# Eight shift rows of the first modulation on TensorE, one column at a time, and four moves on DVE and SP

## What is computed

```python
cond = jax.nn.silu(c)
for l in range(DEPTH):
    m = (cond @ w_mod[l] + b_mod[l]).reshape(bsz, 3, 3, D_MODEL)     # [sublayer, (shift, scale, gate)]
    x = x + 0.5 * m[:, 0, 2][:, None] * swiglu(adaln_in(x, norm_g[l, 0], m, 0), ...)
    h = adaln_in(x, norm_g[l, 1], m, 1) @ w_in[l]
    # mixer: 8 heads of attention beside a short or long convolution, then w_out with gate m[:, 1, 2]
    # second feed-forward with m[:, 2, :]
def adaln_in(x, g, m, i):
    return rmsnorm(x, g) * (1 + m[:, i, 1][:, None]) + m[:, i, 0][:, None]
```

## Time and profile before

| | us |
|---|---|
| median of 3 runs | 1430.19 (1429.68 to 1430.36) |
| profiled execution, its own time | 1432.25 |
| its span | 1430.5 |
| PE busy / PEld busy | 1358.0 / 1294.1 |
| DVE busy / ACT busy | 1088.9 / 692.5 |
| DMA, mean | 213 GB/s |

### The profile page before, as it was taken

One profiled execution on the slowest core, in us unless ns is written; L12 is line 12 of the kernel. 1 busy time (PEld: TensorE's weight loads), 2 busy tenths in 40 slices (PEclk: granted clock), 3 DMA queues, 4 the chain that ended last, 5 costly groups with the idle time before them and its releaser, 6 DMA issues.

```text
span 1430.5 us, 26076 instructions
## 1 busy us (share of the span) xinstructions
PE 1358.0 (95%) x10734; PEld 1294.1 (90%) x10734; DVE 1088.9 (76%) x1835; ACT 692.5 (48%) x1120; POOL 53.9 (4%) x57
## 2 busy tenths in 40 slices
PE   2899999899999999999998999999999989999998
PEld 2899998799999989999998789999997868899998
DVE  6788998887787879888778766565578767677776
ACT  3343435555344354334464544443477756554453
POOL 0000000002000000001000020000010021100000
PEclk9999999999999999999999999999999999999999
DMA  9898758346877576574653055545432325244551
GB/s 393 344 404 324 295 192 325 117 151 274 331 275 295 222 297 267 223 295 191 271 209 138 32 205 205 222 177 214 161 142 84 139 65 186 87 180 177 183 195 65
DMA packets 32182, 305.79 MB, mean 214 GB/s; under 512 B 3480, under 2 KB 5784, under 8 KB 7360
## 3 DMA queue, kind: packets, MB, share of 16 engines
q1 hardware_dynamic: 32064, 304.13, 55.0%
HBM read 303.05 MB, written 1.06 MB: 213 GB/s over the span
## 4 chain that ended last, share of the span: by engine, by line
PE 85%; DVE 6%; ACT 3%; DMA 3%; issue 2%; POOL 1%; SPq 0%; POOLq 0%; DVEq 0%; ACTq 0%
PE bank L690 14%; PE bank L694 14%; PE bank L691 14%; PE bank L864 13%; PE bank L783 7%; PE bank L781 7%; PE bank L788 7%; DMA ring<-in_stream 2%; DVE WL L1856 2%; PE bank L673 1%; PE bank L708 1%; DMA PR<-in_stream 1%; PE bank L937 1%; ACT WH L1283 1%; PE bank L957 1%
## 5 line engine op out<-in xcount | busy, mean ns | idle before, releaser
L1856 DVE TENSOR_TENSOR WL<-ring,WH 128x1024 fp32r<-128x1024 f32 x414 | 495.9, 1221 | 64.2 <-ACT WH L1283 62.1
L1283 ACT ACTIVATE WH<-ring 128x1024 fp32r<-128x1024 f32 x414 | 424.5, 1054 | 145.2 <-DMA ring<-in_stream 55.0
L690 PE MATMUL bank<-XH,WH 128*128 128x256 f32 x1648 | 403.3, 283 | 4.3 <-ACT WH L1283 4.3
L691 PE MATMUL bank<-XL,WH 128*128 128x256 f32 x1648 | 401.5, 282 | 0.0
L690 PEld LDWEIGHTS bank<-XH,WH 128*128 128x128 f32 x1648 | 311.5, 189 | 10.2 <-issue 9.7
L691 PEld LDWEIGHTS bank<-XL,WH 128*128 128x128 f32 x1648 | 311.4, 189 | 0.5 <-issue 0.5
L694 PE MATMUL bank<-XH,WL 128*128 128x256 f32 x1648 | 230.1, 282 | 0.0
L694 PEld LDWEIGHTS bank<-XH,WL 128*128 128x128 f32 x1648 | 210.7, 189 | 0.0
L781 PE MATMUL bank<-GH,WH 128*128 128x256 f32 x840 | 202.6, 279 | 0.1
L783 PE MATMUL bank<-GL,WH 128*128 128x256 f32 x840 | 202.5, 279 | 0.0
L1368 ACT ACTIVATE SG<-bank 128x256 f32<-128x256 f32 x84 | 32.2, 384 | 334.7 <-PE bank L694 330.2
(11 more groups left out here) (321 smaller groups left out, 1601.4 us busy)
## 6 DMA issues: line engine op xcount, KB each, us to landing
ring<-in_stream SPq DMA_DIRECT2D x128, 1536.0 KB, 6.7
scr<-in_stream SPq DMA_DIRECT2D x15, 1536.0 KB, 11.1
PR<-in_stream SPq DMA_DIRECT2D x15, 1536.0 KB, 9.3
att<-in_stream SPq DMA_DIRECT2D x15, 1536.0 KB, 10.0
ring<-in_stream SPq DMA_DIRECT2D x13, 1024.0 KB, 5.0
ring<-in_stream SPq DMA_DIRECT2D x10, 512.0 KB, 3.6
kf_mix<-in_stream SPq DMA_DIRECT2D x2, 1536.0 KB, 16.8
con<-in_consts SPq DMA_DIRECT2D x1, 1680.0 KB, 14.8
```

Of the source, the lines that this page charges most:

```text
L690: pe.matmul(o, part(WH, u, k), XH[:, k, :], start=(k == 0), stop=False)
L691: pe.matmul(o, part(WH, u, k), XL[:, k, :], start=False, stop=False)
L1283: act.activation(part_all(WH, u), raw(u), ACT.Copy).then_inc(*mark("high", u))
L1856: dve.tensor_tensor(part_all(WL, u), raw(u), part_all(WH, u).bitcast(F32), ALU.subtract)\
```

## The change

- Input: the front items are packed otherwise. Scale row k is row 2k, shift row k is row 2k+1, and a shift row now holds eight 128x128 blocks with the condition's features on the partitions. Rows 16 and 17 are the gate rows. `c_cols` holds the condition as eight columns.
- SP: X, the ones and ring slot 0 are issued first, then the 16 rows one by one, the later ones when the row six places before has been read; then the gate rows, into the place of item 0. The waits of mod items 6 and later and of ring slot 2 are on the new marks.
- TensorE: `shift(k)` makes 128 shift values by eight products with one moving column; ACT adds `b_mod`. Products of chunk 0 are made for each k between the shifts. The `keep_warm` calls of the front go.
- DVE: 8 scale rows instead of 16 rows; the norm goes chunk by chunk. The gate rows are read behind the first gating.
- Ends of feed-forwards: DVE's rows of `mod_rows(f, 20, 1)` and the memsets come behind the last gating; `down(21)` waits for it one product later.
- Attention: layer 0's `conv_unit(7)` (but its factor) and `conv_unit(8)`, layer 1's `short_conv(12)`, `z_mul(2)` and two WL splits come behind the first maxima or first probabilities.

```diff
+
+    def front_row(n):
+
+        a = (n % MOD_ROWS) * D
+        return mod_slots[n // MOD_ROWS][:, a:a + D]
+
+    def front_read(i):
+
+        n = range(MOD_ROWS * i, min(MOD_ROWS * (i + 1), 2 * KD))
+        scales, shifts = [j // 2 for j in n if j % 2 == 0], [j // 2 for j in n if j % 2 == 1]
+        gates = [("mod_read", HEAD_MODS - 1)] if i == 0 else []
+        return [("scale_in", k) for k in scales[-1:]] + [("shift_sum", k) for k in shifts[-1:]] + gates
...
+            sp.dma_start(con[:, 0:2 * P], const_d[:, 0:2 * P]).then_inc(*mark("ones_in", n=16))
+            sp.dma_start(X, x_d).then_inc(*mark("x_in", n=16))
+            first = ("ffn", 0, 0)
+            sp.dma_start(slot(first), stream[ITEM_AT[first], :, 0:COLS[first]]).then_inc(sig.sem("slot_landed0"), 16)
+            for j in range(2 * KD):
+                if j >= FRONT:
+                    sp.wait_ge(*at("shift_sum" if j % 2 else "scale_in", (j - FRONT) // 2))
+                a = (j % MOD_ROWS) * D
+                sp.dma_start(front_row(j), stream[ITEM_AT["mod", j // MOD_ROWS], :, a:a + D]).then_inc(*mark(f"mod_landed{j % FRONT}", j, n=16))
+            sp.wait_ge(*at("scale_in", 1))
+            sp.wait_ge(*at("shift_sum", 0))
+            sp.dma_start(mod_slots[0][:, D:ITEM], stream[ITEM_AT["mod", HEAD_MODS - 1], :, D:ITEM])\
+                .then_inc(*mark("gate_rows_in", n=16))
...
+                if name == first or name[0] == "mod" and name[1] < HEAD_MODS:
+                    continue
...
-                        sp.wait_ge(*at("mod_read", p))
+                        for w in front_read(p) if p < HEAD_MODS else [("mod_read", p)]:
+                            sp.wait_ge(*at(*w))
+                        if p < HEAD_MODS:
+                            j = max(j for j in range(2 * KD) if j % FRONT == k)
+                            sp.wait_ge(*at("shift_sum" if j % 2 else "scale_in", j // 2))
...
-                    for k in range(KD):
+                    def shift(k):
+                        take(k % 2, "shift_in", k)
+                        pe.wait_ge(*at(f"mod_landed{(2 * k + 1) % FRONT}", 2 * k + 1))
+                        if k == 0:
+                            pe.wait_ge(*at("c_cols"))
+                        for d in range(KD):
+                            last = pe.matmul(bank[k % 2][:, 0:1], front_row(2 * k + 1)[:, d * P:(d + 1) * P], prm("c_cols", d),
+                                             start=(d == 0), stop=(d == KD - 1))
+                        last.then_inc(*mark("shift_sum", k))
+
+                    def products(k):
                         pe.wait_ge(*at("norm_high", key, k))
                         for a, u in units:
-                            if k == 0:
-                                pe.wait_ge(*at("high", u))
-                            pe.matmul(b[:, a * S:(a + 1) * S], part(WH, u, k), XH[:, k, :], start=(a == 0 and k == 0), stop=False,
-                                      skip_group_check=True)
-                    for a, u in units:
...
+                            for which, w in ((WH, ("high", u)), (WL, low_of(u))):
+                                if k == 0:
+                                    pe.wait_ge(*at(*w))
+                                pe.matmul(b[:, a * S:(a + 1) * S], part(which, u, k), XH[:, k, :],
+                                          start=(which is WH and a == 0 and k == 0), stop=False, skip_group_check=True)
+
+                    def low_products(k):
...
+                    for k in range(KD):
+                        shift(k)
+                        if k > 0:
+                            products(k - 1)
+                        if k > 1:
+                            low_products(k - 2)
+                    products(KD - 1)
+                    low_products(KD - 2)
+                    low_products(KD - 1)
+
...
-                    pe.wait_ge(*at("gated", f, c))
+                    if f == 4 or c < NFF - 1:
+                        pe.wait_ge(*at("gated", f, c))
...
@@ -1613,9 +1654,35 @@
             act.wait_ge(*at("par_in"))
             act.wait_ge(*at("c_in"))
             act.activation(cond[:, :], cond[:, :], ACT.Silu).then_inc(*mark("cond"))
+            act.activation(prm("c_cols", 0, 8), prm("c_cols", 0, 8), ACT.Silu).then_inc(*mark("c_cols"))
+
+            def front_norm():
+                k0, (u0, u1) = ("sub", 0, 0), up_units(0, 0)
+                load_rates()
+                squares(k0, lambda c: [("x_in",)])
+                split_to(u0)
+                root(k0)
+                split_to(u1)
+                for k in range(KD):
+                    act.wait_ge(*at("scale_in", k))
+                    g = prm("norm_g", k)
+                    act.activation(adav[:, 0, 0, k:k + 1], modv[:, KD + k:KD + k + 1], ACT.Identity, scale=g, bias=g)\
+                        .then_inc(*mark("rate_in", k))
+                    act.wait_ge(*at("shift_sum", k))
+                    act.activation(modv[:, k:k + 1], bank[k % 2][:, 0:1], ACT.Identity, bias=prm("b_mod", k))\
+                        .then_inc(*mark("shift_in", k))
+                    if k > 0:
+                        if k == 1:
+                            act.wait_ge(*at("shift_in", 0))
+                        act.wait_ge(*at("shift_in", k - 1))
+                        highs(k0, [k - 1])
+                act.wait_ge(*at("shift_in", KD - 1))
+                highs(k0, [KD - 1])
+                split_to(u1)
+
             for l in range(2):
                 if l == 0:
-                    norm(("sub", 0, 0), lambda c: [("x_in",)], ahead=up_units(0, 0)[1])
+                    front_norm()
                 else:
                     norm(("sub", 1, 0), added("ffn1"), ahead=up_units(2, 0)[1] + 1)
...
@@ -1990,6 +2054,15 @@
                     ends = f < 4 and c == NFF - 1
                     if not ends:
                         split_to(up_units(f, c)[1] + PARTS)
+                    if f == 0 and c == 0:
+                        dve.wait_ge(*at("gate_rows_in"))
+                        for r in range(1, MOD_ROWS):
+                            mod_row(HEAD_MODS - 1, r)
+                    if ends:
+                        mod_rows(f, c - 1, 1)
+                    if ends and f != 1:
+                        link(dve.memset(PR[:, :, 0:PADL], 0.0))
+                        link(dve.memset(PR[:, :, PADL + S:PW], 0.0))
                     mod_rows(f, c, 0)
                     if f == 0:
                         start_step(c)
@@ -1997,10 +2070,8 @@
                         filter_step(c)
                     if c > 0 and not ends:
                         split_to(UNIT_AT["w2", f, c - 1] + PARTS)
-                    mod_rows(f, c, 1)
-                    if f in (0, 2, 3) and c == NFF - 2:
-                        link(dve.memset(PR[:, :, 0:PADL], 0.0))
-                        link(dve.memset(PR[:, :, PADL + S:PW], 0.0))
+                    if f == 4 or c != NFF - 2:
+                        mod_rows(f, c, 1)
...
-            for i in range(HEAD_MODS - 1):
-                for r in range(MOD_ROWS):
-                    mod_row(i, r)
-            mod_row(HEAD_MODS - 1, 0)
-            scale_rates(0, 0)
-            norm_root(("sub", 0, 0))
+
+            def scale_row(k):
+                dve.wait_ge(*at(f"mod_landed{2 * k % FRONT}", 2 * k))
+                w = front_row(2 * k)
+                dve.tensor_tensor_reduce(w, w, cond[:, :], 1.0, prm("b_mod", KD + k), ALU.mult, ALU.add,
+                                         accum_out=modv[:, KD + k:KD + k + 1]).then_inc(*mark("scale_in", k))
+
+            def front_norm():
+                k0, (u0, u1) = ("sub", 0, 0), up_units(0, 0)
+                scale_row(0)
+                split_to(u0)
+                scale_row(1)
+                split_to(u1)
+                norm_root(k0)
+                for k in range(1, KD + 1):
+                    if 1 < k < KD:
+                        scale_row(k)
+                    dve.wait_ge(*at("rate_in", k - 1))
+                    norm_scale(k0, [k - 1])
+                    if k > 1:
+                        norm_lows(k0, [k - 2])
+                norm_lows(k0, [KD - 1])
+
             for l in range(2):
                 if l == 0:
-                    norm_parts_of(("sub", 0, 0), lambda: split_to(up_units(0, 0)[1]))
+                    front_norm()
                     split_to(up_units(0, 1)[1])
-                    dve.wait_ge(*at("gate_rows_in"))
-                    for r in range(1, MOD_ROWS):
-                        mod_row(HEAD_MODS - 1, r)
...
@@ -2242,13 +2327,19 @@
                     split_to(u0 + 6 + PARTS)
                     head_scale("a")
 
+                    def factor(j):
+                        c, role = conv_role(j)
+                        g = PR[:, 11 + c, :]
+                        dve.wait_ge(*at("act_copied", name, j - 1))
+                        dve.wait_ge(*at("product", name, j))
```

(28 more changed lines are left out.)

53 lines of the change are left out of this document (23 added, 30 removed).

## The result

| | before | with the change |
|---|---|---|
| median, us | 1430.28 (1429.68 to 1431.40, 4 runs) | 1438.01 (1437.04 to 1438.74, 4 runs) |
| ratio | | 1.0048 [1.0033, 1.0063] |
| profiled execution, span | 1432.25, 1430.5 | 1438.74, 1436.9 |
| PE busy / PEld busy | 1358.0 / 1294.1 | 1382.2 / 1320.5 |
| mean granted clock | 0.989 | 0.98 |

What follows compares the result with a forecast made beforehand. TensorE was taken to bound the kernel, with 85% of the chain. The terms +0.7 - 3.1 - 2.3 - 4.9 = -9.6 us took the runs' median from 1430.19 to 1420.6, range 1416 to 1434.

Steps and rivals of the forecast that it cites:

- front: Start of the kernel up to chunk 2: chunk 2 at 58.7 instead of 58.0 us, +0.7 (bounds -2.5 and +3).
- ends, maxima of both layers: Work moved behind last gatings and first maxima or probabilities: -3.1, -2.3 and -4.9, together -10.3 us.
- a step: Front, one shift row plus products of chunk 0: 3.4 us at full clock, 5.8 in the first rival.
- The first rival: Clock falls during the front's one-column shift rows: step 5.8, chunk 2 +14.7, total 1434.6 us; chance 0.22.
- The second rival: Front clock falls but weight loads keep their price: step 4.1, chunk 2 +3.5, total 1423.4 us; chance 0.10.
- The load behind the front: Modulation item 6 and ring slot 1 queue from 35.8; chunk 1 starts at 47.6 (was 42.14), slow clock costs 2.6.
- Ends of feed-forwards: Last chunks' gating: TensorE's three waits of 3.3 us go but for one hop each, -3.1 us (bounds 0 and -3.3).
- First maxima: Attentions' first turns start sooner: layer 0 -2.3 us (bounds -1.0, -5.6), layer 1 -4.9 (bounds -1.5, -5.2).

Runs made afterwards that it cites:

- front_only_pad: The changed kernel's front alone, ends of feed-forwards and first maxima as before, with eight more unused parameter columns than the changed kernel: 1428.06 us, ratio 0.9977.
- before_pad16: The kernel before with sixteen unused parameter columns, every tile behind the parameters 64 bytes further: 1417.81 us, ratio 0.9902.
- moves: The kernel before with only the ends of feed-forwards and the first maxima of both attentions moved as in the change: 1421.87 us, ratio 0.9928.
- before_pad: The kernel before with eight unused parameter columns, tiles behind them 32 bytes further: 1435.41 us, ratio 1.0021.
- wide: after_pad with 128 moving columns in each shift product in place of one: 1408.24 us, ratio 0.9835.
- after_pad: The changed kernel with eight more, unused parameter columns: 1417.79 us, ratio 0.9903.
- after: The changed kernel itself, with the whole change against the kernel before: 1438.01 us, ratio 1.0048.
- xh32: The kernel before with eight unused parameter columns and the key norms' tile behind GL, so XH, XL move 32 bytes and GH, GL stay: 1425.21 us.
- ring2_x128: wide with ring slots 1 and 2 issued earlier, tiles behind the parameters 128 bytes further than in the kernel before: 1415.64 us, ratio 0.9889.
- before_g64: The kernel before with sixteen unused parameter columns and an unused sixteen-column tile ahead of SG, GH, GL: 1402.18 us, ratio 0.9799.
- ring2_g64: wide with ring slots 1 and 2 issued earlier and an unused sixteen-column tile ahead of SG, GH, GL: 1394.57 us, ratio 0.9734.

## Why the prediction was wrong, step by step

| term | forecast | measured | from |
|---|---|---|---|
| front | +0.7 | +10.3 | front_only_pad, before_pad16 |
| ends, maxima of both layers | -10.3 | -10.4 | moves |
| 32 bytes | none | +3.1 (profiles: +6.0) | before_pad |

The forecast's sum was -9.6, and the two steps that it lacks are the slow clock in the shift rows (without it the front is +0.8, by `wide`) and the tiles that the new columns push on.

**The front** is the step that failed. "In the new order TensorE does shift(k), then products(k-1)" was right, and "a step is 1.83 + 0.9 + 6 x 0.118 = 3.4" was right for the clock that it assumed (3.49 in `wide`). The reason why it should have that clock was not: I read from the rows that the clock falls behind idle times of 3.7 us and more, and took a TensorE that stands only 0.9 at a time to be safe. It fell at 18.3 with no idle time since TensorE's first product at 9.91. `after_pad` has the same fall; `wide` differs from it in the moving columns alone and keeps the clock up through the same waits. So it was the one-column products. The first rival had the mechanism and its sizes: 3.5 for a shift row (3.41), a step of 5.8 (5.60). It was 3.6 too high at chunk 2 (11.1 for 14.7): the up-projection of chunk 0 ended near 57.6 where it had 61.6, of which seven shorter steps are 1.4, and some 22 records that ran before the clock fell, 0.1 cheaper each, are 2.2. I gave it 0.22; with no row of one-column work longer than 1.9 us, it should have had more.

The second rival (loads keep their price) is out. By the rule of the Trainium skill that the prediction weighed (TensorE: Matmul & The Clock Gate, LDWEIGHTS: columns over 1.2, one figure) a load would take the same at both clocks; these traces have 333 ns at 0.50 (`after`, above) and 192 at 1.00 (`wide`).

**The load behind the front** was forecast from a front that didn't come: in the changed kernel ring slot 1 is there when ACT splits it, from 54.87 on, and TensorE doesn't wait at 57.59. In `wide` it came nearly as worked out: item 6 and slot 1 issued at 35.52 and 35.90 (forecast 35.8), chunk 1 at 46.65 (47.6), the slow clock behind it; the front's term is 1408.24 less (1417.81 - 10.4), +0.8 for +0.7.

**Ends of feed-forwards**: -1.55, -1.35 and the third one's share; forecast 3.1 together. **First maxima**: layer 0 -2.2 (forecast -2.3), layer 1 with the third end -5.2 (forecast 4.9 and about 0.5). The reasons hold: idle time of 1.4 and 0.9 us ahead of the turns (1.2 and 1.1 forecast), no slow clock behind them, small waits in layer 0 (0.89 for the conv gate) that give a part back.

**The place of the tiles** was in no step. The input has eight new parameter columns, and the sum has no term for them; that they move every tile behind them was not seen. What that does alone is shown by `before_pad`. That its down products slow down is measured; why they do is not known.

The three terms make +3.0 by medians, +5.9 with the profiles' 6.0 for the last, and +7.7 was measured. By the profiles the kernel before with eight columns (1438.21) and the changed one (1438.74) differ by 0.5, and their marks at 1021 us by 0.3: there the account closes. By the medians 4.7 us are left; the groups ran on several chips, whose runs of the kernel before differ by 2 us, and I can't settle the rest. Nor is all of the profiles' 6.0 the slower chunk: between 1147 and 1181 us of the old time the changed kernel falls 1.7 further behind and `before_pad` 1.4, as both have one more stretch at the slow clock there (from 1168.6 and 1168.0 on), and neither trace tells whether every execution has it.

The rule of the Trainium skill (TensorE: Matmul & The Clock Gate, Step-by-step: what each phase is for) that TensorE has two read ports, so that loading weights takes nothing from the running product, gives no reason why the distance between tiles counts. These runs show that it does: a product of the up-projection takes 117.4 ns in `xh32` (5.633 / 48) and 118.7 in `before_pad`, and 119.6 in `ring2_x128` (5.740 / 48). What the ports do I can't tell. (By the same page's Back-to-back issue gap an isolated product of 256 columns takes an estimated 109 ns, N / 2.4 + 2.5; 113.3 is the least seen here in a long stream, 8.16 / 72.)

## What to carry to other kernels

A bound engine has a rate as well as a busy share: compare the length of a steady piece of work in both traces before explaining anything else, and be suspicious of every edit that moves tiles, a few columns in a table included. Before judging a change, measure it with the tiles where they were; and when TensorE bounds, try a few unused columns between weights and operands and measure each, since here 8 of them cost 3 us and 16 gained 14, more than any part of the change. A long stretch of one-column products ran at the slow clock here, although the profile called TensorE busy: where more moving columns cost no time, as 128 didn't here, move more than you need.

## What the runs showed of the hardware

- The granted clock fell from 1.00 to 0.50 at 18.3 us while TensorE was busy without a break, with products of one moving column (`after`), and stayed at 1.00 with 128 columns and waits of 0.75 us in each step (`wide`).
- Starts of F32 records at 1.00 lie 112 ns apart with one moving column (`after`, 16 to 18 us) and with 128 (`wide`): up to there the columns cost nothing. At 0.50 one-column records are 213 ns apart, and a weight load takes 333 ns where it takes 192 at 1.00. That the load sets the pace is likely, and not shown.
- A steady stream of fp32r products with 256 columns took between 8.32 and 8.58 us for 72 in the second feed-forward, when nothing but the places of the tiles was changed; moving all tiles together by 64 bytes changed nothing. Which distance is best, and why `before_g64` takes 8.16 in its first feed-forward and 8.48 in its second with the tiles at the same places, is open. Kernels with these places also vary more between executions (1387 to 1397 in `ring2_g64`, 1398 to 1409 in `before_g64`).
